# Low parts of the weights: all on VectorE, none on POOL

## The chip, the cores and the metric

One NeuronCore of a Trainium2 chip runs the whole program. Its engines work from queues of their own and wait for each other by semaphores: PE (TensorE) multiplies, DVE (VectorE), ACT (ScalarE) and POOL (GpSimd) do the elementwise work, and SP (SyncE) issues the loads. The metric is the time of one execution on the device in microseconds (us).

## What is computed

The reference is two transformer-like blocks in fp32 on 256 tokens of width 1024. Cut to what matters:

```python
for l in range(2):                                   # first block, two layers
    h = rms_norm(x, norm_mix[l])
    (m_qk, m_v, m_o, m_i, m_f, r_x, r_g, a_q, a_k, a_v, a_qi, a_ki, a_w, gates) = split(h @ w_in[l])
    y_a = mlstm(m_qk, m_v, m_i, m_f) * sigmoid(m_o)
    y_b = gelu(r_g) * rg_lru(causal_conv(r_x))
    y_c = sparse_attention(rope(a_q), rope(a_k), a_v, rope(a_qi), rope(a_ki), a_w)   # top 64 keys
    x = x + (g_a * (y_a @ w_branch[l, 0]) + g_b * (y_b @ w_branch[l, 1]) + g_c * (y_c @ w_branch[l, 2])) @ w_out[l]
    h = rms_norm(x, norm_ffn[l])
    x = x + (gelu(causal_conv(h @ up_gate)) * (h @ up_value)) @ ffn_down[l]
x = rms_norm(x, norm_final)
h = concat(meta_tokens, x)                           # second block, one layer, 16 + 256 tokens
z, xbc, dt, b, c, hh = split(rmsnorm(h) @ w_in_2)
h = h + concat(ssd(z, xbc, dt), b * causal_conv(c * hh)) @ w_out_2
h = h + mixture_of_experts(rmsnorm(h))               # 4 groups of 4 experts, top 2 within one group
return rmsnorm(h)[16:]
```

## The kernel before

**Weights come in chunks of 1 MB.** A chunk is a tile of 128x2048 fp32. Each goes through four steps: SP loads it into `w_raw`; ACT casts it to the rounded type fp32r (`w_hi`, the high part); then the low part `w_lo = w_raw - w_hi` is made by one TENSOR_TENSOR subtraction; and PE multiplies three times for each product (high x high, high x low, low x high, `product`, L2004 to L2008). The activations are split in the same way (`act_h` and `act_l`, `y_h` and `y_l`).

**Stages.** A layer of the first block has 42 chunks of mixing (`SECTION`: the input projections, then the gates and branches, then the output) and 36 of the feed-forward part, three in each step of a loop. The second block has 32 chunks of mixing (`SECTION_2` and eight for the output, `MIX_2`), then routing, then the experts: 20 passes of six chunks (`MOE`: gate G, up U and down D in two halves each). Three buffers of each kind serve the chunks in turn (`RING`); in the expert stage there are five raw buffers (`RAWS`; `x_t` and `spare_w` among them) and four split ones (`SPLITS`; `w_hi_m` and `w_lo_m` are the fourth).

**The order is written out by hand, for each engine.** In mixing, DVE does for each chunk c: `ahead(c)` and `evacuate(c)` (takes PE's result out of the PSUM bank `main[g % 2]`), then `split(c + 3)` (the low part of a later chunk, L1201 to L1205), then `side(c)`, the rest of the layer's work that goes beside the products: convolution, rope (`rope`, L1287), the gate rows (`gate_rows`, L1307), the scan of the recurrence (L1484 to L1489), index scores and selection (`index_unit`, `select`), attention, the mLSTM. Each queue runs strictly in order. `split(c + 3)` waits for the semaphore `hi_ready`, that is for ACT's high part, which ACT makes after PE has finished chunk c. Its end releases PE's chunk c + 3 and SP's next load into the same raw buffer (`lo_ready`). The second block has the same form: `evacuate_2`, `split_2`, `side_2`; there `side_2(1)` makes the step sizes (L1757 to L1768), `side_2(10)` to `side_2(17)` the decay of the state-space heads (L1693) and `ahead_2` its product (L1703), `side_2(17)` to `side_2(20)` the short convolution (L1807).

**Who makes the low parts.** In mixing, from chunk 3 on, POOL makes those of all chunks whose number is not a multiple of 3 (`pool_splits`), two of three; DVE makes the others. In the feed-forward part DVE makes all. In the expert stage they share each chunk by columns: DVE takes 0 to 1343 (L1836), POOL 1344 to 2047 (L693); `CUT` is 1344, and a chunk is ready when both have counted, so PE and SP wait for two counts (`moe_lower_done`). Otherwise POOL only makes rope's cosine products (L661), the sums of the merged branches (L669), and a few constants.

## Time and profile before

| | us |
|---|---|
| median of three runs | 1795.41 |
| the three runs | 1789.62, 1795.41, 1798.51 |
| the profiled execution | 1790.27 |
| its span, first to last instruction | 1788.5 |

The stages in the profiled execution, by PE's work: mixing of layer 0 from about 28 to 343 us, its feed-forward part to 561; layer 1 the same, to 1107; mixing of the second block to 1383; routing to 1406; experts to 1774; the rest is the last norm. "Busy" counts the time in which an engine executes an instruction, waits excluded; an instruction that is held up inside by another engine counts as busy. The rows further down show, behind each instruction's start and duration, in brackets the idle time of its engine before it and what ended that.

### The profile page before, as it was taken

How to read it: one execution, taken by the hardware profiler on the slowest of the kernel's cores; microseconds unless marked ns; L12 is line 12 of the kernel's file. 1: busy time of each engine (PE TensorE's matmuls, PEld its weight loads, DVE VectorE, ACT ScalarE, POOL GpSimd, SP SyncE). 2: the span in 40 equal slices, each digit the busy share in tenths (PEclk: the TensorE clock that was granted, in tenths of full speed). 3: DMA queues.
4: the chain of work that ended last, by engine and by line, in shares of the span. 5: the costliest groups of instructions: out<-in, count | busy, mean ns of one | idle time of the engine just before them, and what ended most of it. 6: DMA issues, size and time to landing. Idle time of an engine off the chain costs nothing.

```text
span 1788.5 us, 28861 instructions
## 1 busy us (share of the span) xinstructions
PE 1632.9 (91%) x11632; PEld 1515.5 (85%) x11632; DVE 1277.1 (71%) x1456; ACT 948.4 (53%) x982; POOL 716.1 (40%) x236
## 2 busy tenths in 40 slices
PE   3889999799996979999899997799989899999997
PEld 3879989799996969989899997698889787787775
DVE  6598574565556498656365556855994799999997
ACT  5537454454444636555454444455543676767774
POOL 0544436200000444436400000243344399989884
PEclk9999999899998989999999999899999899999999
DMA  7434535555554434534645554334334499999993
GB/s 195 142 95 143 165 119 165 154 180 173 188 187 132 142 95 143 163 119 155 182 146 188 170 187 160 93 120 140 120 126 150 171 344 349 352 339 354 350 352 124
DMA packets 227949, 329.57 MB, mean 184 GB/s; under 512 B 26112, under 2 KB 184704, under 8 KB 227840
## 3 DMA queue, kind: packets, MB, share of 16 engines
q1 hardware_dynamic: 227840, 328.07, 55.8%
q8 instruction: 74, 1.21, 0.3%
q14 instruction: 35, 0.29, 0.0%
HBM read 327.00 MB, written 1.05 MB: 183 GB/s over the span
## 4 chain that ended last, share of the span: by engine, by line
PE 51%; issue 17%; DVE 16%; POOL 13%; ACT 2%; DMA 1%; POOLq 0%; SPq 0%; DVEq 0%; ACTq 0%
PE bank L2006 16%; PE bank L2007 15%; PE bank L2008 15%; POOL w_lo L645 11%; DVE w_lo L1836 5%; DVE w_lo_m L1836 1%; POOL work L661 1%; PE bank L2357 1%; POOL work L669 1%; DMA w_raw<-in_w_in 1%; PE bank L2463 1%; DVE nf L1807 1%; DVE work L1746 1%; DVE work L1222 1%; DVE work L1211 0%
## 5 line engine op out<-in xcount | busy, mean ns | idle before, releaser
L2006 PE MATMUL bank<-act_h,w_hi 128*128 128x256 f32 (+1 forms) x2176 | 627.4, 288 | 41.5 <-DVE act_l L1227 18.6
L2007 PE MATMUL bank<-act_l,w_hi 128*128 128x256 f32 (+1 forms) x2176 | 617.6, 284 | 0.0
L2008 PE MATMUL bank<-act_h,w_lo 128*128 128x256 f32 (+1 forms) x2176 | 616.7, 283 | 0.0
L645 POOL TENSOR_TENSOR w_lo<-w_raw,w_hi 128x2048 fp32r<-128x2048 f32 x71 | 332.3, 4682 | 412.7 <-ACT w_hi L721 242.2
L2006 PEld LDWEIGHTS bank<-act_h,w_hi 128*128 128x128 f32 x2176 | 416.2, 191 | 52.4 <-DVE act_l L1227 21.5
L2007 PEld LDWEIGHTS bank<-act_l,w_hi 128*128 128x128 f32 x2176 | 416.6, 191 | 0.5
L2008 PEld LDWEIGHTS bank<-act_h,w_lo 128*128 128x128 f32 x2176 | 415.6, 191 | 0.0
L1204 DVE TENSOR_TENSOR w_lo<-w_raw,w_hi 128x2048 fp32r<-128x2048 f32 x106 | 247.0, 2331 | 145.5 <-ACT w_hi L721 145.0
L721 ACT CAST w_hi<-w_raw 128x2048 fp32r<-128x2048 f32 x158 | 301.3, 1907 | 78.2 <-PE bank L2008 69.4
L2006 PE MATMUL bank<-y_h,w_hi 128*128 128x256 f32 x704 | 200.6, 285 | 5.2 <-DVE y_l L1552 2.9
L2007 PE MATMUL bank<-y_l,w_hi 128*128 128x256 f32 x704 | 198.1, 281 | 0.0
L2008 PE MATMUL bank<-y_h,w_lo 128*128 128x256 f32 x704 | 197.6, 281 | 0.0
L693 POOL TENSOR_TENSOR w_lo<-w_raw,w_hi 128x704 fp32r<-128x704 f32 x54 | 156.0, 2902 | 21.2 <-ACT w_hi L1081 21.2
L1836 DVE TENSOR_TENSOR w_lo<-w_raw,w_hi 128x1344 fp32r<-128x1344 f32 x54 | 146.0, 2719 | 3.7 <-ACT w_hi L1081 3.7
L2006 PEld LDWEIGHTS bank<-y_h,w_hi 128*128 128x128 f32 x704 | 131.9, 187 | 6.1 <-DVE y_l L1552 3.3
L2008 PEld LDWEIGHTS bank<-y_h,w_lo 128*128 128x128 f32 x704 | 133.0, 189 | 0.0
L2007 PEld LDWEIGHTS bank<-y_l,w_hi 128*128 128x128 f32 x704 | 132.5, 188 | 0.2
L1081 ACT CAST w_hi<-w_raw 128x2048 fp32r<-128x2048 f32 x54 | 103.4, 1917 | 41.2 <-PE bank L2008 28.6
L2006 PE MATMUL bank<-w_hi,xt_h 128*128 128x512 f32 x244 | 98.5, 404 | 0.0
L651 POOL COPY par<-par_all 128x190 f32 x2 | 0.7, 342 | 242.7 <-DVE x_t L1597 229.4
L2007 PE MATMUL bank<-w_lo,xt_h 128*128 128x512 f32 x244 | 96.7, 396 | 0.0
L2008 PE MATMUL bank<-w_hi,xt_l 128*128 128x512 f32 x244 | 96.6, 396 | 0.0
(439 smaller groups left out, 2885.8 us busy)
## 6 DMA issues: line engine op xcount, KB each, us to landing
w_raw<-in_w_in SPq DMA_DIRECT2D x88, 1024.0 KB, 5.5
w_raw<-in_ffn_up SPq DMA_DIRECT2D x48, 1024.0 KB, 5.1
w_raw<-in_e_gate SPq DMA_DIRECT2D x26, 1024.0 KB, 6.3
w_raw<-in_ffn_down SPq DMA_DIRECT2D x24, 1024.0 KB, 4.9
w_raw<-in_e_up SPq DMA_DIRECT2D x23, 1024.0 KB, 5.8
w_raw<-in_e_down SPq DMA_DIRECT2D x23, 1024.0 KB, 5.8
w_raw<-in_w_out SPq DMA_DIRECT2D x16, 1024.0 KB, 5.4
w_raw<-in_w_branch SPq DMA_DIRECT2D x12, 1024.0 KB, 5.0
```

Of the source, the lines that this page charges most:

```text
L645: nc.gpsimd.tensor_tensor(w_lo[c % RING][:], w_raw[c % RING][:], w_hi[c % RING][:].bitcast(F32), ALU.subtract).then_inc(sem[f"lo_ready{c % ...
L661: nc.gpsimd.tensor_tensor(dst, rope_in[i % 2], cos_t[:].unsqueeze(1).to_broadcast([P, 2, T]), ALU.mult).then_inc(sem["rope_cos"], 1)
L669: nc.gpsimd.tensor_tensor(merged[:, b:b + 2, :], merged[:, b:b + 2, :], merge_t[half], ALU.add).then_inc(sem["wb_sum"], 1)
L693: nc.gpsimd.tensor_tensor(lo_m[h][:, CUT:2048], raw_m[i % RAWS][:, CUT:2048], hi_m[h][:, CUT:2048].bitcast(F32), ALU.subtract)\
L721: nc.scalar.copy(w_hi[c % RING][:], w_raw[c % RING][:]).then_inc(sem["hi_ready"], 1)
L1081: nc.scalar.copy(hi_m[i % SPLITS], raw_m[i % RAWS]).then_inc(sem["hi_ready"], 1)
L1204: V.tensor_tensor(w_lo[c % RING][:], w_raw[c % RING][:], w_hi[c % RING][:].bitcast(F32), ALU.subtract).then_inc(sem[f"lo_ready{c % RING}"], 1)
L1222: STT(norm_f[:, k, :], x_t[:, k, :], gains[:, col + k:col + k + 1], sums_r, ALU.mult, ALU.mult).then_inc(sem["scaled"], 1)
L1836: V.tensor_tensor(lo_m[h][:, 0:CUT], raw_m[i % RAWS][:, 0:CUT], hi_m[h][:, 0:CUT].bitcast(F32), ALU.subtract).then_inc(sem[moe_lowered(i)], 1)
L2006: mm(out, a_hi, b_hi, start=first, stop=False, skip_group_check=True)
L2007: mm(out, a_hi, b_lo, start=False, stop=False, skip_group_check=True)
L2008: return mm(out, a_lo, b_hi, start=False, stop=last, skip_group_check=True)
```

## The change

POOL makes no low part any more. `pool_splits` and `CUT` are gone. In mixing DVE makes the low part of every chunk, at the same place in its order at which it made every third one. In the expert stage DVE subtracts all 2048 columns at once, and PE and SP wait for one count for each chunk. What is left to POOL keeps its order.

```diff
--- before.py
+++ after.py
@@ -75,11 +75,6 @@
 DVE_EVACUATES = ("rx", "mqk", "wb", "wo")
 
 
-def pool_splits(c, end):
-
-    return RING <= c < end and c % RING != 0
-
-
 def groups_of(c):
 
     return 2 if SECTION[c][0] == "wb" else 1
@@ -119,7 +114,6 @@
 PASSES = 5 * PER_GROUP
 RAWS, SPLITS = 5, 4
 SCATTER = (5, 6, 7, 2)
-CUT = 1344
 
 
 MOE = [("G", 0, 0), ("G", 0, 1), ("U", 0, 0), ("U", 0, 1)]
@@ -476,7 +470,7 @@
                 eng.wait_ge(sem[moe_landed(i)], n)
 
         def moe_lower_done(eng, i):
-            n = earlier(moe_lowered(i)) + 2 * (i // SPLITS + 1)
+            n = earlier(moe_lowered(i)) + (i // SPLITS + 1)
             if i % SPLITS < RING:
                 need(eng, moe_lowered(i), DEPTH, n)
             else:
@@ -668,8 +662,6 @@
                             need(pool, "evac_dve", L, evacuations(c, True) + half + 1)
                             nc.gpsimd.tensor_tensor(merged[:, b:b + 2, :], merged[:, b:b + 2, :], merge_t[half],
                                                     ALU.add).then_inc(sem["wb_sum"], 1)
-                    if pool_splits(c + RING, MIX):
-                        split(L, c + RING)
 
             pool.wait_ge(sem["par_loaded"], 16)
             pool.wait_ge(sem["setup_act"], 2)
@@ -682,20 +674,7 @@
             nc.gpsimd.tensor_copy(hx[:, :, 0:META], meta[:]).then_inc(sem["meta_ready"], 1)
             nc.gpsimd.tensor_tensor(w_route[:], w_route[:], p2[:, Q_NFF:Q_NFF + KT].unsqueeze(2)
                                     .to_broadcast([P, KT, 20]), ALU.mult).then_inc(sem["moe_consts"], 1)
-            for c in range(MIX_2 - 1):
-                if pool_splits(c + RING, MIX_2):
-                    split(DEPTH, c + RING)
-
-            def moe_split(i):
-
-                h = i % SPLITS
-                need(pool, "hi_ready", DEPTH, MIX_2 + i + 1)
-                nc.gpsimd.tensor_tensor(lo_m[h][:, CUT:2048], raw_m[i % RAWS][:, CUT:2048],
-                                        hi_m[h][:, CUT:2048].bitcast(F32), ALU.subtract)\
-                    .then_inc(sem[moe_lowered(i)], 1)
-
-            moe_split(0)
-            moe_split(1)
+
             mixed_out(pool)
             nc.gpsimd.tensor_scalar(diag[:], ident[0:20, 0:20], p2[0:20, Q_RB:Q_RB + 1], None, ALU.mult)\
                 .then_inc(sem["moe_consts"], 1)
@@ -705,8 +684,6 @@
                            allow_small_or_imprecise_dtypes=True).then_inc(sem["moe_consts"], 1)
             nc.gpsimd.iota(place[:], [[1, SLOTS]], base=0, channel_multiplier=0,
                            allow_small_or_imprecise_dtypes=True).then_inc(sem["moe_consts"], 1)
-            for i in range(2, len(MOE)):
-                moe_split(i)
 
 
         @block.scalar
@@ -1565,11 +1542,9 @@
                     if c == MERGE:
 
                         side(L, c)
-                        if not pool_splits(c + RING, MIX):
-                            split(L, c + RING)
+                        split(L, c + RING)
                     elif c < MIX - 1:
-                        if not pool_splits(c + RING, MIX):
-                            split(L, c + RING)
+                        split(L, c + RING)
                         side(L, c)
                 norm(L, 1)
                 split(L, MIX + 2)
@@ -1833,8 +1808,8 @@
             def moe_split(i):
                 h = i % SPLITS
                 need(dve, "hi_ready", DEPTH, MIX_2 + i + 1)
-                V.tensor_tensor(lo_m[h][:, 0:CUT], raw_m[i % RAWS][:, 0:CUT], hi_m[h][:, 0:CUT].bitcast(F32),
-                                ALU.subtract).then_inc(sem[moe_lowered(i)], 1)
+                V.tensor_tensor(lo_m[h], raw_m[i % RAWS], hi_m[h].bitcast(F32), ALU.subtract)\
+                    .then_inc(sem[moe_lowered(i)], 1)
 
             def lower_tokens(half):
 
@@ -1956,8 +1931,7 @@
                 elif c >= IN_2 + 4:
                     add_out(c)
                 if c + RING < MIX_2:
-                    if not pool_splits(c + RING, MIX_2):
-                        split_2(c + RING)
+                    split_2(c + RING)
                 elif c < MIX_2 - 1:
                     moe_split(c + RING - MIX_2)
                 side_2(c)
```

DVE in a layer, between the gate rows of chunk 4 and rope's first product in chunk 5. Before; the names are tiles, the numbers behind them buffers, ISA and REGISTER_ALU rows are waits on semaphores:

```order
L1472 TENSOR_TENSOR work<-work 128x1024
L422 REGISTER_ALU
L1473 SCALAR_TENSOR_TENSOR work<-work 128x1024
L408 ISA
L1292 TENSOR_TENSOR work<-bank6,sin_t 128x512
L422 REGISTER_ALU
L1296 TENSOR_TENSOR work<-work 128x512
L408 REGISTER_ALU
L1301 TENSOR_TENSOR work<-bank7,sin_t 64x256
L1302 TENSOR_TENSOR work<-work,cos_t 64x256
```

And changed:

```order
L1449 TENSOR_TENSOR work<-work 128x1024
L416 REGISTER_ALU
L1450 SCALAR_TENSOR_TENSOR work<-work 128x1024
L402 REGISTER_ALU
L1181 TENSOR_TENSOR w_lo2<-w_raw2,w_hi2 128x2048
L402 ISA
L1269 TENSOR_TENSOR work<-bank6,sin_t 128x512
L416 REGISTER_ALU
L1273 TENSOR_TENSOR work<-work 128x512
L402 REGISTER_ALU
L1278 TENSOR_TENSOR work<-bank7,sin_t 64x256
L1279 TENSOR_TENSOR work<-work,cos_t 64x256
```

The subtraction of chunk 8 (`w_lo2`) now stands between the recurrence's preparation (L1473, now L1450) and rope (L1292, now L1269).

DVE in the second block, at the end of chunk 1's evacuation and the start of the step sizes. Before:

```order
L1663 SCALAR_TENSOR_TENSOR work2<-bank3,p2,work2 128x271
L1663 SCALAR_TENSOR_TENSOR work2<-bank3,p2,work2 128x270
L1663 SCALAR_TENSOR_TENSOR work2<-bank3,p2,work2 128x269
L1759 SCALAR_TENSOR_TENSOR work2<-work2 16x272
L1760 TENSOR_SCALAR work2<-work2 16x272
L1192 TENSOR_SCALAR work2<-work2 16x272
L1193 RECIPROCAL work2<-work2 16x272
L1194 TENSOR_TENSOR work2<-work2 16x272
```

And changed:

```order
L1638 SCALAR_TENSOR_TENSOR work2<-bank3,p2,work2 128x271
L1638 SCALAR_TENSOR_TENSOR work2<-bank3,p2,work2 128x270
L1638 SCALAR_TENSOR_TENSOR work2<-bank3,p2,work2 128x269
L1609 TENSOR_TENSOR w_lo1<-w_raw1,w_hi1 128x2048
L1734 SCALAR_TENSOR_TENSOR work2<-work2 16x272
L1735 TENSOR_SCALAR work2<-work2 16x272
L1169 TENSOR_SCALAR work2<-work2 16x272
L1170 RECIPROCAL work2<-work2 16x272
L1171 TENSOR_TENSOR work2<-work2 16x272
```

Chunk 4's subtraction (`w_lo1`) now stands between the evacuation and L1759 (now L1734).

DVE in the expert stage, from one product of a pass (`m_hf`) to the next. Before:

```order
L1925 SCALAR_TENSOR_TENSOR m_hf<-m_sg,small_m,bank1 128x512
L1836 TENSOR_TENSOR w_lo_m<-w_raw1,w_hi_m 128x1344
L1836 TENSOR_TENSOR w_lo2<-x_t,w_hi2 128x1344
L1930 TENSOR_TENSOR ht_l<-bank2,ht_h 128x512
L1836 TENSOR_TENSOR w_lo0<-spare_w,w_hi0 128x1344
L1836 TENSOR_TENSOR w_lo1<-w_raw2,w_hi1 128x1344
L1925 SCALAR_TENSOR_TENSOR m_hf<-m_sg,small_m,bank1 128x512
```

And changed:

```order
L1900 SCALAR_TENSOR_TENSOR m_hf<-m_sg,small_m,bank1 128x512
L1811 TENSOR_TENSOR w_lo_m<-w_raw1,w_hi_m 128x2048
L1811 TENSOR_TENSOR w_lo2<-x_t,w_hi2 128x2048
L1905 TENSOR_TENSOR ht_l<-bank2,ht_h 128x512
L1811 TENSOR_TENSOR w_lo0<-spare_w,w_hi0 128x2048
L1811 TENSOR_TENSOR w_lo1<-w_raw2,w_hi1 128x2048
L1900 SCALAR_TENSOR_TENSOR m_hf<-m_sg,small_m,bank1 128x512
```

The order is the same; each subtraction has 2048 columns where it had 1344, and POOL's queue has none.

## Rows read from the trace of the kernel before

**Rows 1.** The page, busy us of each engine, share of the span, instructions:

```profile
PE 1632.9 (91%) x11632; PEld 1515.5 (85%) x11632; DVE 1277.1 (71%) x1456; ACT 948.4 (53%) x982; POOL 716.1 (40%) x236
```

**Rows 2.** Groups by line: shapes, xcount, busy us, mean ns, idle before and releasers:

```profile
L645 POOL TENSOR_TENSOR w_lo<-w_raw,w_hi 128x2048 fp32r<-128x2048 f32 x71 | 332.3, 4682 | 412.7 <-ACT w_hi L721 242.2 <-ACT w_hi L979 170.3
...
L1204 DVE TENSOR_TENSOR w_lo<-w_raw,w_hi 128x2048 fp32r<-128x2048 f32 x106 | 247.0, 2331 | 145.5 <-ACT w_hi L721 145.0
...
L693 POOL TENSOR_TENSOR w_lo<-w_raw,w_hi 128x704 fp32r<-128x704 f32 x54 | 156.0, 2902 | 21.2 <-ACT w_hi L1081 21.2
...
L1836 DVE TENSOR_TENSOR w_lo<-w_raw,w_hi 128x1344 fp32r<-128x1344 f32 x54 | 146.0, 2719 | 3.7 <-ACT w_hi L1081 3.7
```

**Rows 3.** Stages: stretch, length, busy PE, PEld, DVE, ACT, POOL, PEclk, DMA share, GB/s:

```profile
60.00:345.00 285.00, 261.91 (x2078) 250.99 (x2076) 189.25 (x273) 147.56 (x186) 132.07 (x38) 0.97 0.45 138
...
1159.50:1169.00 9.50, 4.91 (x22) 4.95 (x23) 8.97 (x21) 4.24 (x6) 0.00 (x0) 0.50 0.35 110
...
1165.00:1300.00 135.00, 134.11 (x992) 123.89 (x992) 90.41 (x152) 72.55 (x95) 47.45 (x11) 0.98 0.41 125
...
1430.00:1560.00 130.00, 129.14 (x577) 103.33 (x575) 127.90 (x65) 93.38 (x63) 129.13 (x44) 1.00 0.98 349
```

**Rows 4.** Timeline, DVE in layer 0: start us, duration us, instruction, [idle <-releaser]:

```profile
73.88 1.22 DVE L1472 TENSOR_TENSOR work<-work 128x1024 f32<-128x1024 f32 x1 [9.97 <-issue]
...
77.99 4.35 DVE L1296 TENSOR_TENSOR work<-work 128x512 f32<-128x512 f32 x1
...
94.56 0.69 DVE L1296 TENSOR_TENSOR work<-work 128x512 f32<-128x512 f32 x1
...
97.44 4.63 DVE L1321 TENSOR_TENSOR tiny<-tiny,work 4x256 f32<-4x256 f32 x1
...
102.82 0.41 DVE L1324 TENSOR_TENSOR tiny<-work,tiny 4x256 f32<-4x256 f32 x1
...
104.56 2.33 DVE L1484 TENSOR_TENSOR work<-work 128x1024 f32<-128x1024 f32 x1
...
113.68 1.22 DVE L1489 TENSOR_TENSOR work<-work 128x1024 f32<-128x1024 f32 x1
...
154.59 2.68 DVE L1243 SCALAR_TENSOR_TENSOR work<-bank,par,work 128x255 f32<-128x255 f32 x6 [0.36 <-ACT work L750]
```

**Rows 5.** Timeline, PE in layer 0, first instruction after each wait:

```profile
84.65 0.79 PE L2077 MATMUL bank<-work,cst 128*128 128x256 f32 x1 [4.99 <-DVE work L1305]
...
116.53 0.79 PE L2147 MATMUL bank<-work 64*128 64x256 f32 x1 [5.10 <-ACT work L893]
...
244.09 0.62 PE L2114 MATMUL bank<-work,ones 128*128 128x256 f32 x1 [2.59 <-ACT work L822]
...
300.22 0.39 PE L2006 MATMUL bank<-act_h,w_hi 128*128 128x256 f32 x1 [2.01 <-DVE work L1263]
```

**Rows 6.** Timeline, step sizes of the second block, DVE and then PE:

```profile
1145.39 3.03 DVE L1759 SCALAR_TENSOR_TENSOR work<-work 16x272 f32<-16x272 f32 x1 [2.10 <-ACT work L1050]
...
1152.43 7.49 DVE L1198 SCALAR_TENSOR_TENSOR work<-work 16x272 f32<-16x272 f32 x7
...
1159.96 0.43 DVE L1199 SCALAR_TENSOR_TENSOR work<-work 16x272 f32<-16x272 f32 x1
...
1164.09 0.56 PE L2006 MATMUL bank<-act_h,w_hi 128*128 128x272 f32 x1 [6.94 <-DVE work L1663]
```

**Rows 7.** Timeline, short convolution of the second block, DVE and then PE:

```profile
1299.26 9.80 DVE L1807 SCALAR_TENSOR_TENSOR nf<-work,p,nf 128x256 f32<-128x256 f32 x4 [0.99 <-ACT nf L1074]
...
1310.24 1.78 DVE L1807 SCALAR_TENSOR_TENSOR nf<-work,p,nf 128x256 f32<-128x256 f32 x4
...
1334.78 0.48 PE L2408 MATMUL bank<-work,cst 128*128 128x256 f32 x1 [3.30 <-ACT work L1045]
```

**Rows 8.** Timeline, expert stage, POOL in the steady state and PE at the end:

```profile
1533.82 3.01 POOL L693 TENSOR_TENSOR w_lo_m<-x_t,w_hi_m 128x704 fp32r<-128x704 f32 x1
...
1763.46 0.47 PE L2516 MATMUL bank<-cst,m_hf 128*128 128x128 f32 x1 [2.88 <-DVE m_hf L1925]
```

## The prediction

> **What bounds the kernel now.** I read the busy times first, then the instruction groups, then the busy times by stage, and last the timelines around the longest waits of TensorE. TensorE is busy for 91% of the span, VectorE for 71%, POOL for 40% [rows 1]. A kernel like this can only get shorter where TensorE waits or runs at the lower clock, so the question for each removed or added instruction is which wait of TensorE it moves.
>
> The groups tell the price of the work that moves. The same subtraction of 128x2048 takes 4.68 us on POOL and 2.33 us on VectorE; in the expert stage the two shares of one chunk, 704 columns on POOL and 1344 on VectorE, take 2.90 and 2.72 us although they are a third and two thirds of it [rows 2]. Scaled from the whole chunk, they would be 1.61 and 1.53 us. So both are stretched when they run together: 2.90 + 2.72 is 5.6 us of two engines for what VectorE alone does in 2.33.
>
> The timeline of layer 0 shows why [rows 4]. VectorE's addition L1296 takes 0.69 us, but 4.35 in the one case where a POOL subtraction has just begun; the tiny L1321 on 4 partitions takes 4.63, where its like L1324 takes 0.41; L1484 takes 2.33 where L1489, of the same shape, takes 1.22. The reader is to see that these operations, with two inputs in SBUF, end when the POOL subtraction ends: the two engines take turns, an instruction at a time. The Trainium skill says this in "SBUF — State Buffer", section "Who interferes with whom": a VectorE instruction with two SBUF inputs and a GpSimd one that reads SBUF block each other for the whole instruction. By that rule VectorE's operations would all fall back to their short durations, as the sum below takes from the rows alone.
>
> TensorE waits for these very operations. In layer 0 (layer 1 repeats it) it waits 4.99 us for L1305, which follows L1296; 5.10 for ScalarE's L893, which waits for the chain through L1484 to L1489; 2.59 later for ScalarE's L822; 2.01 for L1263 [rows 5]. In the second block it waits 6.94 us behind the step-size chain [rows 6] and 3.30 in the short convolution [rows 7]. In the expert stage it hardly waits: 129.14 of 130 us busy, DMA at 0.98, VectorE and POOL both nearly without a pause [rows 3].
>
> **The change part by part.**
>
> *POOL's whole subtractions go to VectorE:* 26 in each layer, 19 in the second block, 71 in all, at 2.33 us each: 165 us of VectorE work for 332 of POOL work [rows 2]. Each stands between the evacuation of a chunk and the side work of that chunk, and waits there for ScalarE's high part; the side work (rope, recurrence, gate rows, score selection) is queued behind it. SP's next load into the same raw buffer waits for it too, but it comes two chunks ahead of use.
>
> *Layer, 73 to 116 us.* Chunk 7's subtraction falls into the 9.97 us for which VectorE stood idle before L1472 and costs nothing; if that idle time went it would cost 2.33. Chunks 8 and 10 come before L1489: +4.66. The blocked time goes: 4.35 - 0.69 = 3.66, 4.63 - 0.41 = 4.22, 2.33 - 1.22 = 1.11, together 8.99 [rows 4]. L1489 is 4.3 us earlier, and with it the end of the 5.10 us wait; the wait of 4.99 shrinks inside that same gain and isn't counted again.
>
> *Layer, 116 to 160 us.* VectorE is behind here: its idle time before the evacuation L1243 at 154.59 is 0.36 us [rows 4]. Four more subtractions (chunks 11, 13, 14, 16) are 9.3 us and only some 4 to 5 us of blocked time goes. VectorE's lead of 4.3 is used up and TensorE waits for a bank instead; it had itself been late at that point, so some of the lead is left. Bounds: 0 and 4.3; I take 3, since later on VectorE has room again (189.25 of 285 us busy in the stage [rows 3]).
>
> *Layer, rest.* The waits of 2.59 and 2.01 [rows 5] each have one blocked VectorE operation in their chain and get one subtraction put before them. Bounds: 0 and 4.6. I take 3.7, and take off 0.7 for head steps of the mLSTM that now stand behind a subtraction that waits for its high part. Per layer 3 + 3.7 - 0.7 = 6, for both layers **12 us**.
>
> *Second block, head.* L1759 falls from 3.03 to 0.43 and the seven L1198 from 7.49 to 7 x 0.43 = 3.01: 7.1 us [rows 6]. Chunk 4's subtraction stands before them, but inside VectorE's 2.10 us of idle time; without that cover it costs 2.33. The wait of 6.94 shrinks by some 6.5. The clock: TensorE is granted 0.50, the 1.2 GHz level, from 1159.5 to 1169 after that long wait [rows 3]; it works there from 1164.1 on, and the full clock would give back about 2.5. Against it stand five subtractions in chunks 5 to 11 while VectorE evacuates every chunk: I take off 1.5. Sum **7.5 us**, bounds 3 and 9.
>
> *Second block, middle.* One added subtraction of 2.33 stands against one blocked product in each step of the state-space heads, and TensorE is busy for 134.11 of 135 us there [rows 3]. I cost it at nothing. What hides it is one chunk of slack between the weights' product and its use; if that went, a late step would cost up to 2.3, a dozen of them 28.
>
> *Short convolution.* L1807 takes 9.80 us at 1299 and 1.78 at 1310 [rows 7]: 8.0 goes, and a few more blocked operations follow. Two subtractions come in. The wait of 3.30 and the smaller ones around it go. Bounds 3.3 and 8.0; I take **7 us**, near the upper, since VectorE has hardly a pause here and all of its lead arrives.
>
> *Experts.* 120 shares of 704 columns leave POOL, and VectorE's 1344 become 2048. In a run of six chunks VectorE now has 6 x 2.33 = 14.0 us plus about 2.5 of other work, against 6 x 3.01, the turn of a POOL share and the pace of the loads in the steady state [rows 8]. That is less load, but TensorE waits only 0.86 us in 130 [rows 3], 2.3 in the 350 us of the stage. At the end it waits 2.88 for a product that is queued behind two stretched subtractions [rows 8]; that goes. **5 us**, bounds 0 and 9 (with a clock that does not fall at the end).
>
> Here a page speaks against the change: the Trainium skill, "Perfetto Trace Analysis", section "Optimizing Scalar/DVE Operations", says that work may be handed from a saturated VectorE even to GPSIMD, though it adds that the shared port may undo it. By its first half VectorE, at 127.90 of 130 us, should shed work and not take more; the second half is what the rows show. It is the third rival.
>
> *Sum:* 12 + 7.5 + 7 + 5 = 31.5. The profiled execution took 1790.27 us (span 1788.5): 1758.8. The median of the three times is 1795.41, 5 above that execution, the lowest 0.7 below it; I go part of the way and say **1761**.
>
> **Rivals.**
>
> *Second: only part of it is collected.* VectorE's queue is full from 77 to 155 us in each layer, and chunks waiting for their high part hold up side work; then the layers give 2 each, the head of the second block 5, the convolution 4, the experts 2: 15 us, 1775 to 1780. For it: the 0.36 us of idle time. Against it: long idle times elsewhere.
>
> *Third, slower: VectorE becomes the bound.* This holds if the long durations belong to VectorE's operations themselves, or to other traffic, and stay. Then 52 added subtractions in the layers are uncovered where VectorE is full, six per layer or 28 us for both, and five plus a few in the second block another 15: 1790 + 43 = about 1833. In the experts 2.72 x 2048/1344 = 4.14 us per chunk, times six, is 25 us where a run takes 18 now: over 100 us more. It decides as soon as a subtraction takes more than about 2.6 us on VectorE in the experts. Against it: 2.33 for the whole chunk in 106 cases [rows 2].
>
> *Fourth: no change that can be told.* The waits end later on something else (a bank, the loads at 0.98 of the DMA engines) and each gain is handed back: 1785 to 1796. For it: TensorE's 91%.
>
> **How the numbers follow.** Forecast 0.72, second 0.15, fourth 0.08, third 0.05. About 0.5% of the time, 9 us, is what a measurement tells from no change: faster is below 1786.4. The first two lie below it: 0.87; within 0.08; slower 0.05. With the low ends of the bounds (0 + 3 + 3.3 + 0) the gain is 6, with the high ones (2 x 8.9 + 9 + 8 + 9) 44; neither all low nor all high is likely, so the range runs from 1743 to 1786, the forecast and the second rival.
>
> **What would show it.** L1296, L1321, L1759, L1198 and L1807 with their short durations in every case; POOL under 5% busy, VectorE near 75%, since it also saves much of what it gets. TensorE's waits at 1164 and 1335 gone, that at 116 still there but earlier by about 4. New waits of TensorE for the evacuation L1243 near 155 in each layer. In the experts the pace unchanged near 18 us per six chunks. Wrong would be: subtractions on VectorE well over 2.4 us, or new waits of TensorE for a low part.

## The result and the profile after

The changed kernel takes 1743.32 us (median of four runs, 1741.64 to 1744.05) beside 1793.24 of the kernel before: a ratio of 0.9706, 95% interval 0.9684 to 0.9728, some 50 us less. The forecast was 1761, its range 1743 to 1786: right in direction, too small by 18 us and at the lowest end of the range (the ratio on the 1795.41 us from which the forecast was made gives 1742.6). The profiled execution of after has a span of 1740.6 us, 47.9 less than before. In the rows shown here, line numbers of DVE, ACT and PE in after are those of before less 23 to 26.

The page of after, busy us of each engine, share of the span, instructions (before in [rows 1]):

```profile
PE 1620.8 (93%) x11632; PEld 1510.3 (87%) x11632; DVE 1273.9 (73%) x1527; ACT 950.2 (55%) x982; POOL 43.6 (3%) x45
```

VectorE got 71 subtractions more and 120 longer ones, and is busy for 3 us less. Groups of its subtractions, as in [rows 2]: shapes, xcount, busy us, mean ns, idle before:

```profile
L1181 DVE TENSOR_TENSOR w_lo<-w_raw,w_hi 128x2048 fp32r<-128x2048 f32 x158 | 362.8, 2296 | 170.8 <-ACT w_hi L698 170.0
L1811 DVE TENSOR_TENSOR w_lo<-w_raw,w_hi 128x2048 fp32r<-128x2048 f32 x54 | 123.3, 2289 | 15.8 <-ACT w_hi L1058 15.1
```

In the experts the whole chunk takes 2.29 us, less than the 2.72 that two thirds of it took beside POOL.

**A ledger of lead.** Both kernels issue the same 11632 matmuls in the same order, so one can subtract the start of each matmul in after from its start in before. The difference is called the lead below: by how much after is ahead at that point. It was 1.5 us at 84.65 us of before, 11.3 at 121.5, 4.8 at 159, 10.0 at 300 and at the end of mixing in layer 0. Layer 1 adds the same (20.2 up to the second block). In the second block it is 28.5 at 1170, 27.7 at 1290 and 36.8 at the end of mixing; at the first expert product it is 37.9, at the product of the last pass but one 43.2, and at the end 47.8. The steps are worked through further down.

TensorE's waits in layer 0 of after, as in [rows 5] (start, duration, in brackets the wait and what ended it):

```profile
83.19 0.48 PE L2051 MATMUL bank<-work,cst 128*128 128x256 f32 x1 [3.55 <-DVE work L1282]
...
107.26 0.48 PE L2121 MATMUL bank<-work 64*128 64x256 f32 x1 [0.35 <-ACT work L870]
...
139.72 0.58 PE L1980 MATMUL bank<-act_h,w_hi 128*128 128x256 f32 x1 [3.41 <-DVE work L1220]
...
154.22 0.39 PE L1980 MATMUL bank<-w_hi,act_h 128*128 128x256 f32 x1 [0.42 <-DVE work L1220]
...
236.75 0.48 PE L2088 MATMUL bank<-work,ones 128*128 128x256 f32 x1 [0.80 <-ACT work L799]
```

The wait of 5.10 us is down to 0.35, that of 2.59 to 0.80; a new one of 3.41 stands at 139.72, where VectorE evacuates a bank late.

### The profile page after: what moved, and what is told of

Its sections match the earlier page's. It is cut to its first block, busy times and chain, and to the rows that moved or that the text cites. A ratio compares the mean times of both kernels' runs of the same rounds, so it can differ in the third digit from the quotient of the medians.

```text
span 1740.6 us, 28741 instructions
## 1 busy us (share of the span) xinstructions
PE 1620.8 (93%) x11632; PEld 1510.3 (87%) x11632; DVE 1273.9 (73%) x1527; ACT 950.2 (55%) x982; POOL 43.6 (3%) x45
## 4 chain that ended last, share of the span: by engine, by line
PE 61%; issue 27%; DVE 7%; POOL 2%; ACT 1%; DMA 1%; SPq 0%; DVEq 0%; POOLq 0%; ACTq 0%
PE bank L1980 19%; PE bank L1981 18%; PE bank L1982 18%; POOL work L663 1%; POOL work L655 1%; DMA w_raw<-in_w_in 1%; PE bank L2331 1%; DVE w_lo L1609 1%; PE bank L2437 1%; DVE work L1638 1%; DVE work L1199 1%; PE bank L2490 1%; DVE work L1188 0%; DVE work L1195 0%; PE bank L2156 0%
## 5 line engine op out<-in xcount | busy, mean ns | idle before, releaser
L1181 DVE TENSOR_TENSOR w_lo<-w_raw,w_hi 128x2048 fp32r<-128x2048 f32 x158 | 362.8, 2296 | 170.8 <-ACT w_hi L698 170.0
L698 ACT CAST w_hi<-w_raw 128x2048 fp32r<-128x2048 f32 x158 | 301.4, 1908 | 79.1 <-PE bank L1982 70.4
L1811 DVE TENSOR_TENSOR w_lo<-w_raw,w_hi 128x2048 fp32r<-128x2048 f32 x54 | 123.3, 2289 | 15.8 <-ACT w_hi L1058 15.1
L1058 ACT CAST w_hi<-w_raw 128x2048 fp32r<-128x2048 f32 x54 | 103.4, 1917 | 37.4 <-PE bank L1982 37.1
L1609 DVE TENSOR_TENSOR w_lo<-w_raw,w_hi 128x2048 fp32r<-128x2048 f32 x30 | 68.6, 2288 | 33.3 <-ACT w_hi L956 33.3
L1509 DVE SCALAR_TENSOR_TENSOR work<-bank,par,work 128x255 f32<-128x255 f32 (+1 forms) x96 | 41.8, 477 | 58.4 <-ACT work L891 55.1
L956 ACT CAST w_hi<-w_raw 128x2048 fp32r<-128x2048 f32 x30 | 57.1, 1904 | 31.0 <-PE bank L1982 30.9
```

The lines of the kernel that those rows point to most:

```text
L698: nc.scalar.copy(w_hi[c % RING][:], w_raw[c % RING][:]).then_inc(sem["hi_ready"], 1)
L956: nc.scalar.copy(w_hi[c % RING][:], w_raw[c % RING][:]).then_inc(sem["hi_ready"], 1)
L1058: nc.scalar.copy(hi_m[i % SPLITS], raw_m[i % RAWS]).then_inc(sem["hi_ready"], 1)
L1181: V.tensor_tensor(w_lo[c % RING][:], w_raw[c % RING][:], w_hi[c % RING][:].bitcast(F32), ALU.subtract).then_inc(sem[f"lo_ready{c % RING}"], 1)
L1509: ins = STT(ff_c[:, h, s:T], main[0][:, 256 * h:256 * h + T - s], pf[:, bass.ds(F_CW + (2 - s) * 24 + 2 * n + h, 1)], ff_c[:, h, s:T], ALU ...
L1609: V.tensor_tensor(w_lo[c % RING][:], w_raw[c % RING][:], w_hi[c % RING][:].bitcast(F32), ALU.subtract).then_inc(sem[f"lo_ready{c % RING}"], 1)
```

## The experiments

Each kernel is compared with the kernel before, run beside it on the same chip. Where a text below sets one against the changed kernel, the two may have run on different chips; the medians of the kernel before on them are 1792.47 to 1794.57 us. The intervals of all ratios exclude 1.

**p_layers: the layers' mixing alone.** The kernel before, with POOL's part left as it was in the second block and the experts:

```diff
 def pool_splits(c, end):
-    return RING <= c < end and c % RING != 0
+    return end == MIX_2 and RING <= c < end and c % RING != 0
```

> One part alone: only in the mixing stage of the two layers of the first block does VectorE make all low parts; POOL keeps its two of three in the second block and its 704 columns in the experts. Theory (the ledger of the two traces: TensorE's norm matmul at the end of mixing is 10.0 us earlier in each layer, 20.2 us for both): 1773 us beside 1793 of the kernel before, with nothing given back later since the feed-forward stages are the same. My sum before the result had 12 us for this part: 1781. Rival (the stages are not independent, a lead is lost at the hand-over to the second block): 1785 or more.

Measured: 1769.98 us (1768.42 to 1770.31) beside 1794.57, ratio 0.9863 (0.9843 to 0.9883): 24.6 us. In the traces the lead is 21.7 us at the start of the second block and 21.8 at the end. Nothing is given back later.

**p_second: the second block's mixing alone.** The same line with `end == MIX and`.

> One part alone: only in the mixing stage of the second block does VectorE make all low parts. Theory (ledger of the two traces: 7.7 us at the step sizes, 0 in the state-space heads, 8.8 us in the short convolution, 0.6 up to the routing): 17 us, 1776. My sum had 14.5: 1778.5. Rival (the head of the second block gained because it came with a better clock or other loads from the layers): 10 us or less.

Measured: 1776.95 us (1772.84 to 1778.30), ratio 0.9893 (0.9872 to 0.9915): 17.6 us. In its trace the lead grows from -5.1 at the block's start to 3.2 behind the step sizes and 11.2 at the end of mixing: 16.3. (It starts below zero because the layers, which are those of before, took 5 us longer in this execution.)

**p_experts: the experts alone.** The kernel before with the changed kernel's `moe_split`, its count of one and no POOL share.

> One part alone: only in the expert stage does VectorE subtract whole chunks and POOL nothing. Theory (ledger of the two traces: 5.3 us over the nineteen passes, in steps of 0.6 to 0.9 us, and 4.4 us at the last pass where TensorE had waited for a product, 1.2 of them the clock): 9.7 us, 1783.5. My sum had 5: 1788. Rival (the loads, with 0.97 of the DMA engines' time in both, set the pace, and the steps came from the earlier stages): 4 us or less.

Measured: 1783.84 us (1778.17 to 1793.91), ratio 0.9942 (0.9923 to 0.9961): 10.7 us. In its trace the expert stage alone brings 10.0, with the DMA engines busy for 0.95 of the time over the passes (0.97 in before); so the rival, that the loads set the pace, fell. The three parts sum to 24.6 + 17.6 + 10.7 = 52.9 us, the whole brought 50: they add up, within the intervals.

**h_pool3: three subtractions back to POOL where VectorE is full.** The changed kernel with

```diff
+def pool_splits(c, end):
+    return end == MIX and c in (13, 14, 16)
```

> The changed kernel, but POOL makes the low parts of chunks 13, 14 and 16 of each layer again. There VectorE is full in the changed kernel (TensorE waits 3.41 us near 140 us of the span for an evacuation), and its own work is searching maxima and evacuating PSUM banks, which the trace of before shows with the same durations beside a POOL subtraction as without. Theory (only operations with their operands in SBUF are held up, and VectorE is the engine that is late there): three subtractions of 2.29 us leave VectorE's queue, the wait of 3.41 and the half clock behind it go, 4 to 6 us a layer: 1731 to 1735 beside 1743 of the changed kernel. Rival (any POOL subtraction costs VectorE as much as it saves, whatever VectorE runs): 1743 or more.

Measured: 1752.77 us (1747.00 to 1755.78), ratio 0.977 (0.9751 to 0.9789): 9 us slower than the changed kernel. The rival held in the time, and the trace shows why. POOL and then VectorE in layer 0 (start, duration):

```profile
118.56 4.61 POOL L645 TENSOR_TENSOR w_lo<-w_raw,w_hi 128x2048 fp32r<-128x2048 f32 x1 [9.20 <-ACT w_hi L708]
126.73 4.60 POOL L645 TENSOR_TENSOR w_lo<-w_raw,w_hi 128x2048 fp32r<-128x2048 f32 x1 [3.56 <-ACT w_hi L708]
139.51 4.55 POOL L645 TENSOR_TENSOR w_lo<-w_raw,w_hi 128x2048 fp32r<-128x2048 f32 x1 [8.18 <-ACT w_hi L708]
```

```profile
118.08 5.37 DVE L1335 SCALAR_TENSOR_TENSOR work<-work,tiny 128x256 f32<-128x256 f32 x2
...
126.98 0.42 DVE L1351 MAX8 tiny<-work 128x8 f32<-128x256 f32 x1
...
128.96 2.52 DVE L1335 SCALAR_TENSOR_TENSOR work<-work,tiny,cst 128x128 f32<-128x128 f32 x1
...
141.46 4.75 DVE L1191 TENSOR_TENSOR w_lo<-w_raw,w_hi 128x2048 fp32r<-128x2048 f32 x1
```

Each of the three met one operation with two SBUF inputs, which then lasted to POOL's end: 128.96 + 2.52 = 131.48 against 126.73 + 4.60 = 131.33; and 139.51 + 4.55 = 144.06, from where VectorE's own subtraction needs its 2.29. The maxima search in between (MAX8, 0.42) ran on. One hit costs up to 4.6 us where handing over a subtraction saves 2.29. (The row of 5.37 us is two operations merged; the one that was hit ends with it, at 123.45, just behind POOL's 118.56 + 4.61 = 123.17.) My theory was right on which operations collide and wrong that none stood there.

**d_beside: POOL works, and nobody waits for it.** The changed kernel and, in the expert stage,

```diff
+            for i in range(2, len(MOE)):
+                own.settle()
+                need(pool, "hi_ready", DEPTH, MIX_2 + i + 1)
+                own(nc.gpsimd.tensor_tensor(idle_w[:], cst[:, 0:704], cst[:, 0:704], ALU.subtract))
```

> The changed kernel, and in the expert stage POOL makes for each chunk from the third on one subtraction of 128x704 on a table that never changes, into a tile that nobody reads; nobody waits for POOL. Theory (turns: a POOL instruction that reads SBUF and a VectorE instruction with two SBUF inputs exclude each other, nothing else of POOL matters): VectorE's subtraction of a chunk ends 1.6 us later, 2.29 + 1.6, with 0.4 of other work 4.3 us a chunk or 26 us for six chunks where TensorE's pace is 17.1: some 150 us slower, about 1890; at the least 3.0 us a chunk beside POOL, 1763. Rival (what cost time in the kernel before was only that PE and SP waited for POOL's own slow share): 1743, unchanged.

Measured: 1800.37 us (1795.88 to 1801.78), ratio 1.0034 (1.0015 to 1.0053): 57 us slower than the changed kernel, for work that no engine needs. VectorE, then its means in the groups (xcount, busy us, mean ns):

```profile
1505.99 3.44 DVE L1816 TENSOR_TENSOR w_lo<-w_raw,w_hi 128x2048 fp32r<-128x2048 f32 x1
1509.36 3.45 DVE L1816 TENSOR_TENSOR w_lo_m<-x_t,w_hi_m 128x2048 fp32r<-128x2048 f32 x1
1512.73 3.45 DVE L1816 TENSOR_TENSOR w_lo<-spare_w,w_hi 128x2048 fp32r<-128x2048 f32 x1
```

```profile
L1816 DVE TENSOR_TENSOR w_lo<-w_raw,w_hi 128x2048 fp32r<-128x2048 f32 x54 | 170.7, 3178 | 2.6 <-ACT w_hi L1063 2.6
```

So what the removed share cost was not only POOL's slowness but the turn that it took. The size was below my 150: POOL's turn cost VectorE 3.45 - 2.29 = 1.16 us, not 1.6; six chunks take 20.3 us on the average of the passes, against 17.6 in after.

**d_fill: POOL only writes.** The same, with `nc.gpsimd.iota(idle_w[:], [[1, 704]], ...)` in place of the subtraction.

> As d_beside, but POOL's instruction is an index table of 128x704 that it writes and for which it reads nothing. Theory (only a POOL instruction that reads SBUF takes turns with VectorE): VectorE's subtractions stay at 2.29 us and the time at 1743. Rival (any POOL instruction beside VectorE, also one that only writes, holds it up): as slow as d_beside in the same measure as its instruction is long.

Measured: 1743.30 us (1742.55 to 1744.14), ratio 0.971: the changed kernel's time. POOL and VectorE in the groups:

```profile
L691 POOL IOTA idle_w<- 128x704 f32 x118 | 85.0, 721 | 284.9 <-ACT w_hi L1064 194.7 <-ACT w_hi_m L1064 90.2
```

```profile
L1817 DVE TENSOR_TENSOR w_lo<-w_raw,w_hi 128x2048 fp32r<-128x2048 f32 x54 | 123.3, 2288 | 15.7 <-ACT w_hi L1064 14.8
```

118 POOL instructions of 0.72 us that read nothing leave the subtraction at 2.288 us. It is POOL's reading that VectorE waits for. (It is also another and a shorter instruction, 0.72 against 2.94 us, but a quarter of those 57 us would show.) The page "SBUF — State Buffer" of the Trainium skill, section "Who interferes with whom", says just this, that a GpSimd instruction which only writes is no obstacle to a VectorE instruction with two SBUF inputs; the trace agrees.

**x_cut: a smaller POOL share.** The kernel before with

```diff
-CUT = 1344
+CUT = 1792
```

> The kernel before, but in the experts POOL takes 256 columns of each chunk instead of 704, VectorE 1792 instead of 1344. Theory (turns: the cost of a chunk is the two shares one after the other, VectorE's 2.33 x 1792/2048 = 2.04 and POOL's 1.61 x 256/704 = 0.59, 2.6 us where TensorE's pace is 2.86): the passes no longer lose, nearly all of what the experts alone gave, 1784 to 1786 beside 1794. Rival (what costs is that POOL takes part at all): 1794, no change.

Measured: 1783.50 us (1778.99 to 1794.53), ratio 0.993 (0.9903 to 0.9957), as p_experts and as the theory had it; by the ledger the expert stage brings 10.0 us here too. A stretch of the stage (stretch, length, busy PE, PEld, DVE, ACT, POOL, PEclk, DMA, GB/s):

```profile
1450.00:1600.00 150.00, 150.00 (x680) 122.13 (x679) 133.80 (x81) 107.27 (x72) 92.85 (x53) 1.00 0.97 357
```

The passes have the 17.1 us for six chunks of the kernel after. So POOL may take part where both turns together stay below TensorE's pace: by the theory's estimate they are 2.6 us a chunk here and 1.53 + 1.61 = 3.1 in before, beside 2.86. No third cut was run.

**s_exp256: how near VectorE is to its limit in the experts.** The changed kernel, and behind each subtraction

```diff
+                if i >= 2:
+                    own.settle()
+                    own(V.tensor_tensor(beside_w[:, 0:256], cst[:, 0:256], cst[:, 0:256], ALU.subtract))
```

> The changed kernel, and VectorE makes one more operation of 128x256 on a table, some 0.42 us, after each subtraction of the expert stage; nobody waits for it. VectorE has 2.33 us of subtraction and 0.42 of other work in a chunk, TensorE 2.86, so 0.1 of slack. Theory (VectorE has little slack left in the experts and the change stands close to its own limit): 3.2 us a chunk where VectorE runs out, about 0.3 too much in 118 chunks: 25 to 45 us slower, 1770 to 1790. Rival (VectorE's queue has slack enough since it is only 87% busy and chunks are buffered four deep): within 5 us of 1743.

Measured: 1743.11 us (1740.86 to 1745.51), ratio 0.9714: no difference, and the rival held. 118 operations of 0.415 us found room. I had worked out 0.1 us of slack a chunk from durations of 2.33; but in after an operation that follows starts 2.21 us after a subtraction's start, and over the passes VectorE is idle for 322.6 - 285.5 = 37 us (the row of after further down), a third of a us for each of the 111 chunks in that stretch.

```profile
L1812 DVE TENSOR_TENSOR w_lo<-w_raw,w_hi 128x2048 fp32r<-128x2048 f32 x54 | 123.2, 2282 | 3.8 <-ACT w_hi L1059 3.8
...
L1816 DVE TENSOR_TENSOR beside_w<-cst 128x256 f32<-128x256 f32 x118 | 49.0, 415 | 0.0
```

The idle time before the first group falls from 15.8 us to 3.8, and over the passes VectorE is busy for 318.7 of 322.6 us: the slack is nearly used up.

**s_mid: the edit that I costed at nothing, doubled.** The changed kernel, with the subtraction of chunks 12 to 20 of the second block made twice:

```diff
+                if 12 <= c <= 20:
+                    step(V.tensor_tensor(w_lo[c % RING][:], w_raw[c % RING][:], w_hi[c % RING][:].bitcast(F32),
+                                         ALU.subtract))
```

> The changed kernel, but in the second block VectorE makes the low parts of chunks 12 to 20 twice over, 2.3 us more for each of nine chunks in the stretch of the state-space heads, where I had costed the added subtractions at nothing. Theory (one chunk of slack and VectorE 67% busy there hide it): 0 to 3 us, 1743 to 1746. Rival (a late step costs what it is late): up to 9 x 2.3 = 21 us, 1750 to 1764.

Measured: 1761.17 us (1755.16 to 1763.61), ratio 0.9793 (0.9746 to 0.9839): 18 us slower. Held against after, matmul by matmul, 19 us go in the state-space heads, and the time is inside the rival's range: the cover holds for the one added subtraction and not for a second. But the loss isn't two us at each step. TensorE's waits from 1170 to 1290 are 11 us in all (what for, sum, times, longest):

```profile
PE bank L2334 <- DVE work L1681: 9.0, 4, 4.4
PE bank L2334 <- ACT work L1010: 2.0, 2, 1.8
```

The other 8 us go behind three of these waits, where TensorE is granted 0.50: from 1194.4 to 1204.7, from 1249.0 to 1252.4 and from 1272.9 to 1279.7 us. In after no part of that stage is below 1.00. So about half of the nine extra subtractions stayed hidden, and the clock nearly doubled the price of what did not.

**v_order: a try at a better order.** The changed kernel, with `select(L, 1, 1)` taken out of `side(L, 11)` and, in VectorE's order of a layer:

```diff
+                    elif 10 <= c <= 16:
+                        if c > 10:
+                            split(L, c + RING - 1)
+                        if c == 12:
+                            select(L, 1, 1)
+                        if c == 16:
+                            split(L, c + RING)
+                        side(L, c)
```

> A try at a better version: the changed kernel with another order on VectorE in each layer: from chunk 10 to 16 the subtraction comes one chunk later, and the second half of the index selection stands behind the evacuation of chunk 12. Theory (TensorE's wait of 3.41 us near 140 us is VectorE's queue in a jam up to 157 us, with about a us of idle time behind it): the wait goes, part of it comes back at the evacuations of chunks 13 and 14, and the half clock behind the wait is saved or not: 1 to 4 us a layer, 1735 to 1741. Rival (the jam is only shifted): 1743.

Measured: 1740.76 us (1738.82 to 1742.34), ratio 0.9696 (0.9668 to 0.9723), not to be told from the changed kernel, though inside the theory's 1735 to 1741. At the end of the two layers its lead over before is 20.5 us, beside 20.2 of after: the trace is on the side of the rival, that the jam is only shifted. The wait has another place and another name, a low part that now comes late:

```profile
148.23 0.57 PE L1988 MATMUL bank<-act_h,w_hi 128*128 128x256 f32 x1 [2.70 <-DVE w_lo L1181]
```

**v_gated: POOL only where nothing collides.** The changed kernel, with POOL making chunks 14 and 16 of each layer at chosen moments:

```diff
+                    if pool_splits(c + RING, MIX):
+                        if c + RING == 14:
+                            need(pool, "idx_used", L, 6)
+                        else:
+                            need(pool, "lo_ready0", L, 15 // RING + 1)
+                        split(L, c + RING)
```

> A try at a better version, the idea of h_pool3 with the collisions taken out: POOL makes the low parts of chunks 14 and 16 of each layer again, but starts chunk 14 only when VectorE has finished the index scores (the search for maxima follows, one input, then an evacuation that reads PSUM), and chunk 16 only when VectorE has made chunk 15 (evacuations and a row maximum follow). Theory (only two-input operations on SBUF collide): two subtractions of 2.29 us leave VectorE's jam and nothing is stretched, the wait of 3.41 us falls to about 1.2 and half of what is lost behind it is kept: 2 to 4 us a layer, 1735 to 1739. Rival (some two-input operation still meets POOL, or PE waits for POOL's slower 4.6 us): 1743 or more.

Measured: 1736.16 us (1733.87 to 1738.03), ratio 0.966 (0.9627 to 0.9693). It is the fastest of all: its six runs lie below all twelve of the three kernels at 1743. POOL, VectorE and TensorE:

```profile
130.10 4.63 POOL L645 TENSOR_TENSOR w_lo<-w_raw,w_hi 128x2048 fp32r<-128x2048 f32 x1 [20.67 <-DVE work L1339]
140.28 4.63 POOL L645 TENSOR_TENSOR w_lo<-w_raw,w_hi 128x2048 fp32r<-128x2048 f32 x1 [5.56 <-DVE w_lo L1195]
```

```profile
133.93 0.94 DVE L1360 TENSOR_SCALAR work<-work 128x256 f32<-128x256 f32 x1
...
141.24 2.67 DVE L1234 SCALAR_TENSOR_TENSOR work<-bank,par,work 128x255 f32<-128x255 f32 x6
143.83 1.28 DVE L1381 SCALAR_TENSOR_TENSOR work<-bank,work 128x512 f32<-128x512 f32 x2
```

```profile
137.98 0.39 PE L1997 MATMUL bank<-act_h,w_hi 128*128 128x256 f32 x1 [0.16 <-DVE work L1234]
```

The evacuations, whose other operand is a PSUM bank, keep their 2.67 and 1.28 us beside POOL, and TensorE's wait falls from 3.41 to 0.16. Behind it the clock stays at 1.00 from 137.9 to 144.9 us, where after had 0.50. At the end of the two layers the lead over before is 29.2 us, 9.0 more than after has there; the other stages are alike. This is what h_pool3 had meant to do. It also hands over two chunks and not three, and no run separates that from the waits that place them.

## Why the prediction was right in direction and too small

**What bounds the kernel, and the mechanism: right.** Two engines take turns, and d_beside and d_fill show it directly. What failed is the sum. In the lead of the trace it should have been 31.5 us and was 47.8: 20.2 in the layers where 12 was forecast, 7.5 in the head of the second block as forecast, 9.1 in the convolution for 7, 1.1 up to the experts for 0, and 9.9 in the experts for 5. The layers, the convolution and the experts each lie above their upper bounds (17.8, 8.0 and 9). Layer 0 of after, to be held against [rows 4]:

```profile
93.10 1.13 DVE L1273 TENSOR_TENSOR work<-work 128x512 f32<-128x512 f32 x1
...
95.31 0.41 DVE L1298 TENSOR_TENSOR tiny<-tiny,work 4x256 f32<-4x256 f32 x1
...
100.69 1.21 DVE L1461 TENSOR_TENSOR work<-work 128x1024 f32<-128x1024 f32 x1
101.94 2.44 DVE L1463 TENSOR_TENSOR_SCAN work<-work 128x256 f32<-128x256 f32 x4
104.41 1.22 DVE L1466 TENSOR_TENSOR work<-work 128x1024 f32<-128x1024 f32 x1
```

**Layers, 12 forecast, 20.2 measured: the term that was mis-sized.** Three things in it.

First, I summed blocked time in L1296, L1321 and L1484 and stepped over the scan between them, which in before reads

```profile
106.92 6.72 DVE L1486 TENSOR_TENSOR_SCAN work<-work 128x256 f32<-128x256 f32 x4
```

and 2.44 after. That is 4.28 us more on the way to L1489, which came 9.3 us earlier instead of 4.3. I took its 6.72 us for its own, since I had no short one beside it. The rest is nearly even: L1319, which I had also passed over, falls from 1.52 to 0.41 us, and two of the additions L1273 (1.13 and 0.96 us, 0.69 when free) lose 0.7, since they meet rope's cosine product, which POOL still makes; I had expected the short duration in every case. Such a product (L661, 104.23 to 105.81 us) and not a subtraction had held L1484 too; that its 1.1 us were gained is luck of the new timing.

Second, I gave the clock a price in the second block but none in the layers. Two stretches at the 1.2 GHz level are gone with the long waits ahead of them, the one behind 84.65 is half as long (to 87.3 instead of 90.7 us), and one came. Before, then after (stretch, length, busy PE, PEld, DVE, ACT, POOL, PEclk, DMA, GB/s):

```profile
114.60:121.40 6.80, 4.87 (x19) 4.09 (x20) 6.32 (x11) 5.35 (x7) 1.27 (x1) 0.50 0.24 81
```

```profile
107.30:114.00 6.70, 6.70 (x53) 6.28 (x54) 6.30 (x11) 3.88 (x5) 1.29 (x1) 1.00 0.55 159
138.50:145.30 6.80, 5.58 (x26) 5.58 (x27) 6.70 (x12) 1.53 (x2) 0.00 (x0) 0.50 0.33 84
```

The lead grows by 2.0 us in the first and shrinks by 2.3 in the new one; the one behind 244.09 gives 1.6.

Third, the clamp. I had the lead capped by VectorE's queue near 155; it was, at 139.72 and 154.22. Of 11.3 us, 6.5 are lost again (3.5 in the wait, 2.3 in the clock behind it, the rest near 154), and 4.8 stayed where I had 3. So the scan and the first clock gain were mostly handed back, and what they left is 1.8. For the rest of the layer, 3.0 net was forecast and 5.3 came: 0.6 near 165 us, 1.8 of the 2.59 wait, 1.6 of clock, 2.2 at L1263, less 1.1 near 270. That last is the loss that I had put at 0.7, of mLSTM steps behind a subtraction that waits for its high part: in after TensorE waits 0.46 us at 260.38 for L1413, which stands behind a subtraction of 2.81 us that had itself waited 0.49 for ScalarE.

**Second block.** The head: 7.5 forecast, 8.3 measured, less 0.8 up to 1290, so 7.5. L1759 fell to 0.42 and the seven L1198 to 3.21; the wait of 6.94 is 0.98 (6.0 gained), and the clock behind it gave 2.3:

```profile
1130.55 3.21 DVE L1175 SCALAR_TENSOR_TENSOR work<-work 16x272 f32<-16x272 f32 x7
...
1137.93 0.37 PE L1980 MATMUL bank<-act_h,w_hi 128*128 128x272 f32 x1 [0.98 <-DVE work L1638]
```

The state-space heads: 0 forecast, 0 measured, and s_mid shows that the next 2.3 us a step would not have been free. The convolution: 7 forecast, 9.1 measured up to the end of mixing, over my bound of 8.0; L1807's 9.80 us became 1.79. I had read the blocked time of that one group and, as in the layers, put too little on those behind it: two pairs of L1749 took 3.80 and 3.70 us before, at 1321.37 and 1329.85, and take 0.88 now. Another 1.1 comes up to the first expert product, where I had nothing.

**Experts, 5 forecast, 9.9 measured: mis-sized too.** I took what the passes could give from TensorE's idle time. The same matmuls from the first pass to the last, before and after:

```profile
1429.80:1757.90 328.10, 326.21 (x1463) 261.54 (x1462) 326.00 (x171) 232.75 (x156) 312.52 (x110) 1.00 0.97 347
```

```profile
1391.90:1714.50 322.60, 322.60 (x1462) 262.85 (x1461) 285.51 (x172) 232.43 (x156) 0.00 (x0) 1.00 0.97 352
```

Before, TensorE is idle for only 1.9 us, yet the stretch is 5.5 us longer. The rest of the waiting does not show as idle time. The records of matmuls overlap, 0.39 us long and 0.23 apart, so a product that starts 0.65 us late shows 0.49 idle and one that starts 0.25 late shows none or 0.02; other records are 0.50 long instead of 0.39. At the end 3.2 us came with the wait, as forecast, and 1.4 behind it, where TensorE had the clock at 0.66 from 1763 to 1768 before and has 1.00 now. And "the pace unchanged" was wrong: on the average of the passes it fell from 17.87 to 17.58 us, with 17.1 in every pass that has nothing but its products. The turns had set it, not the loads, whose share is 0.97 in both.

**The third rival** (VectorE becomes the bound) fell with the subtractions at 2.29 us. Its mechanism is real all the same: in d_beside the long durations stay and VectorE makes whole chunks, and that costs 57 us. By the Trainium skill's "Perfetto Trace Analysis", section "Optimizing Scalar/DVE Operations", a saturated VectorE may shed work even to GPSIMD, unless the shared port undoes it; p_experts and d_beside show that here the port does undo it, h_pool3 and v_gated that it depends on what stands beside it. **The second** was right that VectorE's jam to 155 takes most of the layers' lead. **The fourth** (no change that can be told) fell with the measured interval, 0.9684 to 0.9728.

**The reference.** The sum was made against an execution of 1790.27 us, near the lowest. The kernel before has run 52 times, from 1789.2 to 1808.0 us; the three kernels at 1743 (the change, d_fill, s_exp256), whose layers are as in the change, twelve times, from 1740.9 to 1745.5. p_layers, with POOL's low parts only behind the layers, scatters over 1.9 us in four runs; p_experts, with POOL's work in the layers as before, over 15.7 in twelve. So a good part of the scatter goes with POOL's work in the layers, though not all scatter does: s_mid has no low part on POOL and scatters over 8.5 us in four runs. The one profile that I read was a lucky one, as the last section shows.

## What to carry to other kernels

Before you hand a VectorE operation to POOL, count not POOL's duration against VectorE's but the turns: every VectorE operation with two SBUF inputs that meets a POOL instruction which reads SBUF is held to its end. Hand over only where VectorE reads PSUM, searches maxima or reduces, and start POOL by a semaphore that VectorE itself gives at that place; a `hi_ready` that arrives some time isn't enough. When you sum blocked time, go over every instruction of the chain and compare it per element with its own arithmetic, also where no short twin stands beside it; and take what a saturated engine can give from the pace of start to start, not from idle rows. Give each long wait of TensorE the price of the lower clock behind it as well: in s_mid 11 us of waits cost 19.

## What the runs showed of the hardware

**A collision depends on 1 or 2 us.** p_experts has the layers of before, instruction for instruction, yet in its profiled execution they are 13 us slower. In layer 0 from 121 to 159 us alone it loses 10, some 7 of them by VectorE's lateness. Its VectorE and POOL there:

```profile
126.78 4.08 DVE L1283 TENSOR_TENSOR work<-work 128x512 f32<-128x512 f32 x1
...
134.75 3.96 DVE L1335 SCALAR_TENSOR_TENSOR work<-work,tiny,cst 128x128 f32<-128x128 f32 x1
...
148.68 4.73 DVE L1191 TENSOR_TENSOR w_lo<-w_raw,w_hi 128x2048 fp32r<-128x2048 f32 x1
```

```profile
125.60 4.71 POOL L645 TENSOR_TENSOR w_lo<-w_raw,w_hi 128x2048 fp32r<-128x2048 f32 x1 [7.49 <-ACT w_hi L708]
133.96 4.60 POOL L645 TENSOR_TENSOR w_lo<-w_raw,w_hi 128x2048 fp32r<-128x2048 f32 x1 [3.65 <-ACT w_hi L708]
146.74 4.53 POOL L645 TENSOR_TENSOR w_lo<-w_raw,w_hi 128x2048 fp32r<-128x2048 f32 x1 [8.18 <-ACT w_hi L708]
```

Three hits, which cost VectorE 3.4, 3.6 and 2.5 us. In before's profile the same three POOL subtractions begin at 128.36, 136.72 and 149.50, the first of them just behind the addition that was hit here, and cost it 0.6, 1.3 and 0. Most of the rest is lost where TensorE, late behind VectorE, is granted the lower clock (0.81 on the mean from 149 to 158 us, 1.00 in before from 141 to 160). That the collisions make all of the scatter is not shown, only that these two executions differ by them.

**One input can be held too.** TENSOR_SCALAR L1360 of v_gated has a single SBUF input and took 0.94 us instead of 0.29, up to POOL's end (134.73). The hit of 1.3 us in before was such a one too, beside the POOL subtraction from 136.72 to 141.32:

```profile
139.83 1.64 DVE L1369 TENSOR_SCALAR work<-work 128x256 f32<-128x256 f32 x1
```

The page "SBUF — State Buffer" of the Trainium skill, section "Who interferes with whom", lists `tensor_scalar` and copies as able to take the shared pair; the trace agrees. The same section says that TENSOR_REDUCE doesn't; in before one ran inside a POOL subtraction that lasted from 149.50 to 154.14 and kept the 2.29 us that it also takes in after, where POOL is idle:

```profile
149.50 4.64 POOL L645 TENSOR_TENSOR w_lo<-w_raw,w_hi 128x2048 fp32r<-128x2048 f32 x1 [8.19 <-ACT w_hi L721]
...
150.43 1.28 DVE L1390 SCALAR_TENSOR_TENSOR work<-bank,work 128x512 f32<-128x512 f32 x2
151.74 2.29 DVE L1395 TENSOR_REDUCE tiny<-work 128x8 f32<-128x2048 f32 x1
```
